# Two of the three FFN projections as 2x2 block products by Strassen's algorithm

## What is computed

```python
h = rms_norm(x, norm_ffn_pre[l])
f = (jax.nn.silu(h @ w_ffn_gate[l]) * (h @ w_ffn_up[l])) @ w_ffn_down[l]
x = x + rms_norm(f, norm_ffn_post[l])
```

## Time and profile before

| | |
|---|---|
| median of 3 runs | 829.38 us (828.52 to 830.69) |
| span of the profiled execution | 827.4 us |
| TensorE busy | 816.6 us, 99% |
| VectorE busy | 353.0 us, 43% |
| ScalarE busy | 304.7 us, 37% |
| GpSimd busy | 40.0 us, 5% |
| DMA | 84.16 MB, 102 GB/s |
| first FFN matmul of 256 tokens | 460.26 us |
| first FFN matmul of the loop | 484.15 us |
| first down matmul | 701.78 us |

### The profile page before, as it was taken

The page is one execution under the profiler, slowest core; times in us unless marked ns, Lnnn a source line. Parts: engine busy times, 40 slices in busy tenths (PEclk is TensorE's granted clock), DMA queues, the critical chain, the costliest instruction groups (busy, mean ns, idle before and its releaser), DMA issues.

```text
span 827.4 us, 10167 instructions
## 1 busy us (share of the span) xinstructions
PE 816.6 (99%) x3952; PEld 673.3 (81%) x3952; DVE 353.0 (43%) x516; ACT 304.7 (37%) x574; POOL 40.0 (5%) x96
## 2 busy tenths in 40 slices
PE   7999999999999999999999999999999999999997
PEld 6988777777788888888888988888888888888885
DVE  4742565566344522525655443333333333522122
ACT  5742555555445324334334242233222332412110
POOL 1100000243000000000001000000000000000000
PEclk9999999999999999999999999999999999999999
DMA  9543221311311333334271133333322232622011
GB/s 322 168 129 109 74 79 52 103 52 51 103 51 51 103 102 103 101 102 147 107 254 52 51 102 102 101 101 101 97 82 82 93 126 102 244 80 84 1 51 51
DMA packets 67782, 84.16 MB, mean 102 GB/s; under 512 B 3217, under 2 KB 61089, under 8 KB 67746
## 3 DMA queue, kind: packets, MB, share of 16 engines
q1 hardware_dynamic: 67712, 83.65, 30.9%
q10 hardware_dynamic: 34, 0.01, 0.0%
HBM read 81.54 MB, written 2.11 MB: 101 GB/s over the span
## 4 chain that ended last, share of the span: by engine, by line
PE 97%; DMA 1%; DVE 1%; ACT 0%; issue 0%; SPq 0%; DVEq 0%; POOLq 0%; POOL 0%; ACTq 0%
PE pair L988 90%; PE pair L1079 1%; PE pair L1062 1%; PE pair L1089 1%; PE pair L994 1%; PE pair L1069 1%; PE pair L1093 1%; DMA g_mem_b<-in_norm_mem 1%; PE pair L1015 0%; DVE mem_in L738 0%; PE pair L1110 0%; DVE wo_lo L351 0%; ACT wo_hi L346 0%; PE pair L1100 0%; PE pair L1141 0%
## 5 line engine op out<-in xcount | busy, mean ns | idle before, releaser
L988 PE MATMUL pair<-h2T_hi,w_hi 128*128 128x512 f32 (+1 forms) x384 | 142.7, 372 | 0.0
L988 PE MATMUL pair<-h2T_lo,w_hi 128*128 128x512 f32 (+1 forms) x384 | 142.6, 371 | 0.0
L988 PE MATMUL pair<-h2T_hi,w_lo 128*128 128x512 f32 (+1 forms) x384 | 142.6, 371 | 0.0
L988 PE MATMUL pair<-hT_hi,w_hi 128*128 128x512 f32 x336 | 136.5, 406 | 0.0
L988 PE MATMUL pair<-hT_lo,w_hi 128*128 128x512 f32 x336 | 131.3, 391 | 0.0
L988 PE MATMUL pair<-hT_hi,w_lo 128*128 128x512 f32 x336 | 131.3, 391 | 0.0
L351 DVE TENSOR_TENSOR w_lo<-raw,w_hi 128x1024 fp32r<-128x1024 f32 x69 | 84.3, 1222 | 97.1 <-ACT w_hi L346 96.9
L346 ACT ACTIVATE w_hi<-raw 128x1024 fp32r<-128x1024 f32 x70 | 73.9, 1055 | 90.7 <-PE pair L988 89.3
L701 ACT ACTIVATE w_hi<-raw 128x1024 fp32r<-128x1024 f32 x40 | 42.4, 1061 | 147.3 <-PE pair L988 147.3
L950 DVE TENSOR_TENSOR w_lo<-raw,w_hi 128x1024 fp32r<-128x1024 f32 x40 | 49.0, 1226 | 85.5 <-ACT w_hi L701 85.5
L988 PEld LDWEIGHTS pair<-h2T_hi,w_hi 128*128 128x128 f32 x384 | 72.3, 188 | 12.6
(11 more groups left out here) (151 smaller groups left out, 1089.1 us busy)
## 6 DMA issues: line engine op xcount, KB each, us to landing
raw<-in_w_in SPq DMA_DIRECT2D x42, 512.0 KB, 4.7
raw<-in_w_ffn_gate SPq DMA_DIRECT2D x22, 512.0 KB, 4.7
raw<-in_w_ffn_up SPq DMA_DIRECT2D x22, 512.0 KB, 4.8
raw<-in_w_ffn_down SPq DMA_DIRECT2D x22, 512.0 KB, 3.7
raw<-in_w_mem_kv SPq DMA_DIRECT2D x8, 512.0 KB, 7.0
raw<-in_w_branch_a SPq DMA_DIRECT2D x8, 512.0 KB, 4.1
raw<-in_w_out SPq DMA_DIRECT2D x8, 512.0 KB, 4.1
x_in<-in_x SPq DMA_DIRECT2D x4, 512.0 KB, 9.7
```

The costliest lines, as they stand in the source:

```text
L988: ins = pe.matmul(dst, a, b, start=first and n == 0, stop=last and n == 2)
```

## The change

The first pass (two gate, two up tiles) is kept, with the up tiles first. For the ten other pairs of tiles, a pair's up and gate columns are the two block rows, the two halves of the contraction the two block columns, and the two halves of the tokens the block columns of the right side:

up(half 0) = A11 B11 + A12 B21, gate(half 0) = A21 B11 + A22 B21, and the same with B12, B22 for half 1.

Seven products P1 to P7 (the Winograd form) replace eight. Four sums of weights S1 to S4 are made for each pair by GpSimd, each 128 x 1024 elements; four sums of activations T1 to T4 once, by VectorE, with B11 and B21 joined to plain float32 by GpSimd and B12 and B22 by VectorE. Each product is taken for two tiles of 128 columns (i = 0, 1), so a pair has OPS = 14 operand tiles of 4 steps x 128 columns and 14 block products of 12 matmuls with 256 moving columns. ScalarE and VectorE split each operand into one of seven slots, six products ahead.

Partial results stay in PSUM: bank A of a tile gathers P1, then P6, then P7 on top; ScalarE copies it out after each (U1, U2, U3). VectorE adds the other banks (`block_out`), eight times a pair. GpSimd's sums wait for the fetched gate chunk (S1) and up chunk (S2) and for their old contents' last use. The next up chunk is fetched after S4 and four splits of this pair, the next gate chunk after twelve splits.

f is kept in float32 and split in the down stage into nine slots (`down_f_hi`, `down_f_lo`), two tiles of it in the last pair. The order of down's token tiles becomes 0, 1, 3, 2. The gain row of the last norm is fetched ahead of the down weights.

```diff
+def products():
+    return [("P1", "A11", "B11", "A"), ("P2", "A12", "B21", "B"), ("P6", "S2", "T2", "A"), ("P5", "S1", "T1", "C"),
+            ("P7", "S3", "T3", "A"), ("P4", "A22", "T4", "D"), ("P3", "S4", "B22", "C")]
...
@@ sync
+            with sp.Fori(2, PAIRS + 1) as j:
+                sp.wait_ge(sums_ready, 4 * j - 4)
+                sp.wait_ge(ops_split, OPS * j - 2 * OPS + 4)
+                load_columns(up_v, UP, up_in, j)
+                sp.wait_ge(ops_split, OPS * j - 2 * OPS + 12)
+                load_columns(gate_v, GATE, gate_in, j)
...
@@ gpsimd
+            pool.wait_ge(out_full, TT)
+            pool.wait_ge(turned_split, E_V + 4)
+            for b in ("B11", "B21"):
+                hi, lo = h2[b]
+                pool.tensor_tensor(plain[b][:, :, :], hi[:, :, :].bitcast(F32), lo[:, :, :].bitcast(F32), ALU.add)\
+                    .then_inc(plain_ready, 1)
+            def weight_sums(j, first=False):
+                for n, (out_, a, op, b) in enumerate((("S1", "A21", ALU.add, "A22"), ("S2", "S1", ALU.subtract, "A11"),
+                                                      ("S3", "A11", ALU.subtract, "A21"), ("S4", "A12", ALU.subtract, "S2"))):
...
+                    if not first:
+                        pool.wait_ge(ops_split, OPS * j - 2 * OPS + (8, 6, 10, 14)[n])
+                    pool.tensor_tensor(sums[out_][:, :, :], block_of(a), block_of(b), op).then_inc(sums_ready, 1)
+            pool.wait_ge(rows_turned, E_V + 2 * TT)
+            weight_sums(1, first=True)
+            with pool.Fori(2, PAIRS + 1) as j:
+                weight_sums(j)
...
@@ scalar
+            act.wait_ge(plain_ready, 6)
+            t_hi("T2")
+            act.wait_ge(ffn_full, 1)
+            operand_hi(1, 3)
+            t_hi("T1")
...
+            def pair_of_tiles(j, first=False, last=False):
+                for n in range(OPS):
+                    if n > 0:
+                        act.wait_ge(product_done, OPS * j - OPS + n)
...
+                    if n in (1, 2):
+                        keep("U1", n - 1)
+                    elif n in (5, 6):
...
+                        keep("U2", n - 5)
+                    elif n in (9, 10):
+                        keep("U3", n - 9)
+                    if n < 8:
+                        operand_hi(j, n + 6)
+                    elif not last:
+                        operand_hi(j + 1, n - 8)
+                    elif n in (8, 10):
+                        split_hi(act, at_stream[("down", (n - 8) // 2)])
+                    elif n in (9, 11):
+                        down_f_hi((n - 9) // 2)
+                    if n == 13:
+                        silu_gate(j, 0)
+                silu_gate(j, 1)
...
@@ vector
             split_lo(dve, done)
             done += 1
+            for m in range(3):
+                operand_lo(1, m)
             h2_lo(TT - 1)
...
+            dve.wait_ge(turned_split, E_V + 2 * TT)
+            dve.wait_ge(plain_ready, 2)
+            plain_of("B12")
+            plain_of("B22")
+            t_sum("T1", "B12", "B11", 5)
+            t_sum("T2", "B22", "T1", 6)
+            t_lo("T2", 1)
+            operand_lo(1, 3)
+            t_sum("T3", "B22", "B12", 7)
+            t_sum("T4", "B21", "T2", 8)
+            t_lo("T1", 2)
+            first_f(0)
+            operand_lo(1, 4)
+            first_f(1)
+            operand_lo(1, 5)
+            t_lo("T3", 3)
+            t_lo("T4", 4)
+            def pair_of_tiles(j, last=False):
+                for n in range(OPS):
+                    if n in (3, 4):
+                        dve.wait_ge(product_done, OPS * j - OPS + n)
+                        dve.wait_ge(f_ready, 2 * j - 4 + n)
+                        block_out(n - 3, up_out, 0, "B", "U1")
+                    elif n in (9, 10):
...
+                        block_out(n - 9, gate_out, 1, "C", "U3")
+                    elif n in (11, 12):
...
+                        block_out(n - 11, gate_out, 0, "D", "U3")
+                    elif n == 13:
...
+                        block_out(0, up_out, 1, "C", "U2")
+                    if n < 8:
+                        operand_lo(j, n + 6)
+                    elif not last:
+                        operand_lo(j + 1, n - 8)
...
+                    if n == 13:
+                        f_out(j, 0)
+                dve.wait_ge(product_done, OPS * j)
+                block_out(1, up_out, 1, "C", "U2")
+                f_out(j, 1)
...
@@ tensor
+            def product(j, m, first):
+                name, a, b, bank = products()[m // 2]
+                i = m % 2
+                pe.wait_ge(ops_split, OPS * j - OPS + m + 1)
+                if first and name == "P1" and i == 1:
+                    pe.wait_ge(f_ready, 1)
...
+                (whi, wlo), (xhi, xlo) = op_slot[m % SLOTS], h2[b]
+                fresh = name not in ("P6", "P7", "P3")
+                for k in range(4):
+                    ins = three(bank_of(bank, i)[:, 0:2 * P], whi[:, k, :], wlo[:, k, :], xhi[:, k, :], xlo[:, k, :],
+                                fresh and k == 0, k == 3, onto=not fresh)
+                ins.then_inc(product_done, 1)
+            for m in range(OPS):
+                product(1, m, True)
+            with pe.Fori(2, PAIRS + 1) as j:
+                for m in range(OPS):
+                    product(j, m, False)
```

More of the change, by code:

```diff
@@ L63 @@
 PAIR_OF = (2, 0, 1, 3)
+DOWN_ORDER = (0, 1, 3, 2)
+PAIRS = FT // 2 - 1
+OPS = 14
+SLOTS = 7
 WARM_UP = (30, 0, 3)
@@ L112, in plan @@
     stream += [("out", k) for k in range(4, KT)]
-    stream += [("ffn", e) for e in range(2 * FT)]
+    stream += [("ffn", e) for e in range(4)]
     stream += [("down", k) for k in range(FT)]
@@ L688, in _ @@
             split_hi(act, done)
             done += 1
+            act.wait_ge(out_full, TT)
+            for m in range(3):
+                operand_hi(1, m)
             h2_hi(TT - 1)
[L693 to L720, removed]
+            act.wait_ge(plain_ready, 6)
+            t_hi("T2")
+            act.wait_ge(ffn_full, 1)
@@ L721, in _ @@
+            pair_of_tiles(1, first=True)
+            with act.Fori(2, PAIRS) as j:
+                pair_of_tiles(j)
+            pair_of_tiles(PAIRS, last=True)
+            for k in range(2, FT):
+                split_hi(act, at_stream[("down", k)])
+                down_f_hi(k)
             for t in range(TT):
@@ L959, in _ @@
-            for i in range(4):
-                ffn_step(0, i)
-            with dve.Fori(1, FT // 2 - 1) as f:
-                for i in range(4):
-                    ffn_step(f, i)
-            for i in range(4):
-                ffn_step(FT // 2 - 1, i, last=True)
-            done = at_stream[("down", 4)]
-            while done < len(stream):
-                split_lo(dve, done)
-                done += 1
+            dve.wait_ge(turned_split, E_V + 2 * TT)
+            dve.wait_ge(plain_ready, 2)
@@ L970, in _ @@
+            pair_of_tiles(1)
+            with dve.Fori(2, PAIRS) as j:
+                pair_of_tiles(j)
+            pair_of_tiles(PAIRS, last=True)
+            for k in range(2, FT):
+                split_lo(dve, at_stream[("down", k)])
+                down_f_lo(k)
             dve.wait_ge(gain_loaded["ffn_post"], 16)
@@ L987, in three @@
                 for n, (a, b) in enumerate(pairs):
-                    ins = pe.matmul(dst, a, b, start=first and n == 0, stop=last and n == 2)
+                    ins = pe.matmul(dst, a, b, start=first and n == 0, stop=last and n == 2,
+                                    skip_group_check=onto)
                 return ins
```

250 lines of the change are left out of this document (181 added, 69 removed).

## The result

The changed kernel takes 844.35 us, median of four runs (841.68 to 845.95), for 828.95 of the kernel before beside it: 1.0177 times as long, 95% interval 1.0143 to 1.021. That is 15.4 us more, where the prediction's single value had 8. The profiled execution spans 844.2 us, 16.8 more than before.

What follows compares the result with a forecast made beforehand. TensorE's column count was taken as the bound. Gain -16, steady loop +12, start +11.3 and clock +1 made +8 us on the profiled 827.4, so 835.4; with the median 2.0 over that, about 837 us, range 820 to 847.

Steps and rivals of the forecast that it cites:

- the forecast's own mechanism: FFN stage: GpSimd sums of 2.37 us block VectorE, slowing steady rounds and pair 1's start; 832 to 842 us, chance 0.45.
- rival C: Steady loop: same mechanism, costlier sums (2.56 us) or fetches 0.6 us longer each round; 844 us, chance 0.15.
- the steady loop: FFN pairs: fetch, sums, held splits and VectorE's queue make 21.6 us against TensorE's 20.1; 8 x 1.5 = 12 us lost.
- What bounds the kernel, and the gain: FFN matmuls: TensorE is the bound; 168 narrow matmuls take 20.13 us a pair for 21.76, gaining 16 us in all.
- The exclusion: SBUF read path: VectorE work with two SBUF inputs and GpSimd tensor operations exclude each other by whole instructions; sum 2.37 us.
- Rivals A: FFN loop: quick sums of 1.90 to 2.1 us, so TensorE bounds steady pairs; 823 us, chance 0.16.
- B: SBUF read path: free whenever asked for, or held in short turns, so all is hidden; 813 us, chance 0.10.
- D: FFN loop: sums of 2.1 to 2.3 us, about -3 to +4 us; 828 us, chance 0.14.
- The start: Pair 1: VectorE's queue and six GpSimd operations delay TensorE's second block product to near 497 us, losing 11.3 us.
- The clock: TensorE behind a 7 us gap: the lowered granted clock adds 1 us (0 to 2).
- The down stage: Splitting f there costs nothing: some 8 us of room against a delay under 1.5 us.
- The signs it named: FFN: VectorE subtractions far over 0.69 us, sums 2.4 or longer, TensorE gap 5 to 9, rounds 21 to 22.

Runs made afterwards that it cites:

- experiment 1: Changed kernel, GpSimd forming only eight of the 1024 elements of each weight sum for pairs 2 to 9: 826.65 us, ratio 0.9939 to the kernel before.
- Experiment 4: Changed kernel with all block sums and plain blocks on VectorE and the start reordered: 814.18 us, ratio 0.9829 to the kernel before.
- experiment 5: Kernel before, its 512-column FFN loop cut into halves of 256 columns, nothing else: 841.9 us, ratio 1.015.
- experiment 2: Changed kernel, pairs 2 to 9: eight-element sums, then four full GpSimd subtractions into an unused place: 841.7 us, ratio 1.0143 to the kernel before.
- experiment 7: Changed kernel, next gate chunk fetched after fourteen splits instead of twelve: 852.43 us, ratio 1.0295 to the kernel before.
- experiment 3: Changed kernel, pairs 2 to 9: eight-element sums, each behind two write-only GpSimd fills: 824.79 us in a single run, 824.51 repeated, ratio 0.9938.

## Why the prediction held, and where not

**The number.** Forecast 837, measured 844.35: the way is right and the time lies in 820 to 847, but outside the 832 to 842 given for the forecast's own mechanism. The increase is about twice the one forecast (15.4 us for 8), and the time is the one that rival C named. Of the 7.4 us between 837 and 844.35, the steady loop makes 6.7.

**What bounds the kernel, and the gain.** Right. 960 steps of 226.7 ns against 1680 of 119.8 to 120 give 16.0 us (experiments 1, 4 and 5). Experiment 4 gets 15 of them.

**The exclusion.** Right, and the step on which all hung. Whole instructions take turns: 2.23 and 2.55 us for 0.68. The value taken for a sum, 2.37 us, was measured at 2.40; the slower 512-element row was the nearer one, also for the two sums with a single named input. Rivals A (sums of 1.9 to 2.1 us), B (no exclusion that counts) and D (2.1 to 2.3 us) fall with it.

**The steady loop: the right mechanism, the mis-sized term.** The step that was off is "8 x 1.5 = 12 us lost". Predicted 21.6 us a round; measured 22.45.

| part of the round | predicted | measured |
|---|---|---|
| fetch, release to use | 5.0 | 5.58 |
| first two sums | 4.8 | 5.00 |
| subtractions held by sums 3 and 4 | 5.1 | 5.63 |
| VectorE's queue to the release | 6.7 | 6.24 |
| sum, us | 21.6 | 22.45 |

The fetch was sized by the median landing of 4.2 us, with 0.3 us for the hand-over. The held stretch left out that the fourth sum also waits for a subtraction (2.86 us for 2.40). Over rounds 3 to 10 this is 8 x (2.23 - 1.5) = 5.9 us more than the 12 predicted, and round 2, which the prediction thought hidden, adds 0.9: 18.7 for 12. Rival C named one of the places, "fetches 0.6 us longer each round"; the fetch was 0.58 longer, the sums were not 2.56 us. That alone would have been 8 x 0.58 = 4.6 us, not the 7 that C's 844 counts: the rest came from the held stretch, the first two sums and round 2, less 0.5 us of VectorE's queue. That the time fell on C's number is in part luck.

**The start.** Predicted 11.3 us before the second block product and 1 behind it, 12.3; measured 10.2 and 2.2, 12.4. The total agrees because one term was too large and the other too small by as much, which is luck. TensorE's timeline of the changed kernel around it:

```profile
471.60 1.09 PE L1200 MATMUL pair<-ident,y 128*128 128x128 f32 x8 [0.84 <-DVE y L873]
474.89 0.48 PE L1193 MATMUL pair<-B_hi,w_hi 128*128 128x256 f32 x1 [2.20 <-DVE w_lo L366]
475.17 0.42 PE L1193 MATMUL pair<-B_lo,w_hi 128*128 128x256 f32 x1
...
492.20 0.28 PE L1193 MATMUL pair<-B_hi,op_lo 128*128 128x256 f32 x1
497.50 0.55 PE L1193 MATMUL pair<-B_hi,op_hi 128*128 128x256 f32 x1 [5.02 <-DVE f L1097]
497.84 0.42 PE L1193 MATMUL pair<-B_lo,op_hi 128*128 128x256 f32 x1
498.06 0.42 PE L1193 MATMUL pair<-B_hi,op_lo 128*128 128x256 f32 x1
```

What stretches the early work, in VectorE's timeline:

```profile
468.12 3.42 DVE L873 SCALAR_TENSOR_TENSOR y<-x,rstd,g_ffn_pre_b 128x1024 f32<-128x1024 f32 x1 [2.19 <-POOL rstd L544]
471.47 3.37 DVE L366 TENSOR_TENSOR w_lo<-raw,w_hi 128x1024 fp32r<-128x1024 f32 x1
```

As predicted, the last normalised rows and the last FFN split stand behind GpSimd's plain blocks, each held by whole GpSimd operations (3.42 and 3.37 us for 1.28 and 1.22), and the second block product waits on VectorE's product f. Four more operations of VectorE are held by the weight sums before it (T1 3.45, T2 3.31, T2's lo 2.23, one operand's lo 2.89); the six lose 11.8 us over their own length, where the prediction had 13.5. TensorE resumes at 497.50, in an execution that is 1.71 us late from its beginning; so it is 35.52 us into the stage, where 23.89 + 1.44 = 25.3 would have been unhindered, and 497 without the 1.71 would have been 36.7.

**The clock.** Mis-sized: 1 us (0 to 2) predicted. Window of the changed kernel, columns as above:

```profile
497.40:502.30 4.90, 4.80 (x22) 4.84 (x23) 4.90 (x7) 2.47 (x6) 0.00 (x0) 0.50 0.12 42
```

After the 5.02 us gap the granted clock is 0.50, the 1.2 GHz level, until 502.3. Some 21 matmuls step 0.21 to 0.22 us apart for 0.12; with the slower restart that is 2.2 us, the whole of what is lost behind the gap. It is also at the lower level after the shorter gaps around 471 to 475 us, until 478.4, which costs 16 x 0.09 = 1.5 us there. Those 1.5 us are not lost to the total, since TensorE has to wait before the second block product in any case. Five other profiled executions with the same code up to this place show it (experiments 1, 2 and 7, and both of 3). In three of them, experiments 1 and 2 and the repeated run of 3, the clock does not fall there. The window behind the 2.20 us gap in experiment 1:

```profile
476.90:480.40 3.50, 3.46 (x27) 3.39 (x28) 3.46 (x6) 0.00 (x0) 0.00 (x0) 1.00 0.62 178
```

And in the changed kernel:

```profile
474.90:478.40 3.50, 3.50 (x17) 3.50 (x18) 3.46 (x6) 0.00 (x0) 0.00 (x0) 0.52 0.64 200
```

The gap before the second block product is 6.3 us in those three, and 3.8 to 5.0 us in the three in which the clock falls. In all six it ends 35.46 to 35.53 us into the stage: VectorE sets that time, and not TensorE's clock.

**The down stage.** Right: 125.6 us from the first down matmul to the end, before and after. The later splits are under the matmuls.

**The signs it named** were there: subtractions of 512 far over 0.69 us, sums of 2.4, a gap of 5.0, just inside 5 to 9, released by VectorE, short waits for lo operands. The rounds were not 21 to 22 but 22.4.

## What to carry to other kernels

When work moves to GpSimd, price it by what it does to VectorE's two-input work as well as by its own length: in experiment 2 four subtractions of 2.4 to 2.7 us a round cost 18 us although no operand waited for their values, and the real sums on VectorE, at 1.22 us each, cost about 1 us in all, none of it in the steady rounds. When a transfer is released by the consumer's own progress, write the whole circle down, release, landing, sums, splits, release, and compare it with the bound engine's round; each part that is rounded down by half a microsecond is paid in every round. A reduction in columns is worth its share only at the same matmul width.

## What was not expected of the hardware

- Write-only GpSimd work leaves VectorE alone: fills of 128x1020 (0.95 us each, 8 a round) beside subtractions of at most 0.694 us.
- After the same short gaps the granted clock fell in some executions and not in others: behind gaps of 0.84 and 2.20 us it fell to the 1.2 GHz level in three of six profiled executions (the changed kernel, the single run of experiment 3, experiment 7) and stayed at 1.00 in the three others. Behind the gap of 3.8 to 6.3 us it fell each time, for 1.5 to 2.2 us lost. A loss that is followed by a wait which another engine ends is not added to the time.
- A 256-column matmul keeps its pitch of 119.8 to 120 ns pass after pass, so two of them are 13 ns longer than one of 512, in a stream of 240 us as in the short first pass (experiment 5: 12.8 us over 960 pairs).
